# Down weights of the experts in rows of 16 KB over two ring slots, and inner features in neighbouring pairs

## What is computed

```python
def expert_block(args):
    xblk, e = args                       # tokens routed to expert e
    hid = jax.nn.silu(xblk @ w_gate[e]) * (xblk @ w_up[e])   # w_gate, w_up: 1024 x 512
    return hid @ w_down[e]                                   # w_down: 512 x 1024
...
y = jnp.zeros((t, d), xf.dtype).at[sorted_tok].add(contrib)  # weighted by the router, 2 experts a token
```

## Time and profile before

| | us |
|---|---|
| median of three runs (2711.89 to 2713.6) | 2712.69 |
| the profiled execution's own time | 2713.97 |
| its span, first to last instruction | 2712.2 |
| TensorE busy in the span | 2504.5 (92%) |
| VectorE busy | 1291.7 (48%) |
| ScalarE busy | 866.9 (32%) |
| mean traffic of the DMA engines | 263 GB/s |

### The profile page before, as it was taken

One profiled execution on the slowest core, in us unless ns is written; L12 is line 12 of the kernel. 1 busy time (PEld: TensorE's weight loads), 2 busy tenths in 40 slices (PEclk: granted clock), 3 DMA queues, 4 the chain that ended last, 5 costly groups with the idle time before them and its releaser, 6 DMA issues.

```text
span 2712.2 us, 39463 instructions
## 1 busy us (share of the span) xinstructions
PE 2504.5 (92%) x16084; PEld 1855.5 (68%) x16085; DVE 1291.7 (48%) x2254; ACT 866.9 (32%) x1474; POOL 294.3 (11%) x376
## 2 busy tenths in 40 slices
PE   7999899988898988998899999989999999989998
PEld 4664433443784433343699888879989988888997
DVE  6563323222664323221554675565455467555545
ACT  3241111110342111110344444444444444444443
POOL 0210100000000010000000212320010011233001
PEclk9989999999998999999899999999999999999999
DMA  9987999999774999999755444335646544334372
GB/s 390 343 323 320 420 419 418 412 420 418 242 280 198 420 420 419 414 420 420 278 200 185 143 125 136 124 124 198 197 155 202 187 137 156 119 116 154 132 240 79
DMA packets 253288, 712.09 MB, mean 263 GB/s; under 512 B 14514, under 2 KB 171954, under 8 KB 196786
## 3 DMA queue, kind: packets, MB, share of 16 engines
q1 hardware_dynamic: 249474, 704.94, 68.9%
q10 hardware_dynamic: 2208, 2.60, 0.3%
q0 software_dynamic: 1424, 1.98, 0.2%
HBM read 705.52 MB, written 1.05 MB: 261 GB/s over the span
## 4 chain that ended last, share of the span: by engine, by line
PE 62%; DMA 22%; issue 6%; DVE 5%; POOL 2%; ACT 2%; SPq 1%; ACTq 0%; DVEq 0%; POOLq 0%
DMA ring<-in_e_w_up_dram 19%; PE w L869 17%; PE w L1131 11%; PE y L909 9%; PE w L871 9%; DMA ring<-in_ada_w_dram 3%; PE w L1150 2%; PE w L1417 2%; PE y L776 1%; PE y L1183 1%; DVE wsp L1526 1%; POOL arena L2820 1%; PE w L1402 1%; PE w L971 1%; ACT wsp L1516 1%
## 5 line engine op out<-in xcount | busy, mean ns | idle before, releaser
L1526 DVE TENSOR_TENSOR wsp<-ring,wsp 128x1024 fp32r<-128x1024 f32 x470 | 578.8, 1237 | 400.8 <-ACT wsp L1516 400.3
L869 PE MATMUL w<-hh,wsp 128*128 128x256 f32 (+1 forms) x4800 | 634.0, 285 | 1.0 <-DVE wsp L1526 0.6
L869 PEld LDWEIGHTS w<-hh,wsp 128*128 128x128 f32 (+1 forms) x4800 | 602.8, 191 | 24.4 <-issue 11.9
L1516 ACT CAST wsp<-ring 128x1024 fp32r<-128x1024 f32 x470 | 487.9, 1045 | 389.1 <-PE w L871 208.5
L1131 PE MATMUL w<-ring,arena 128*64 128x512 f32 x2016 | 461.4, 600 | 85.1 <-DMA ring<-in_e_w_up_dram 80.1
L1131 PEld LDWEIGHTS w<-ring,arena 128*64 128x64 f32 x2016 | 154.9, 137 | 353.0 <-issue 351.2
L871 PE MATMUL w<-hl,wsp 128*128 128x256 f32 (+1 forms) x2400 | 336.6, 283 | 0.0
L871 PEld LDWEIGHTS w<-hl,wsp 128*128 128x128 f32 (+1 forms) x2400 | 309.5, 192 | 0.0
L909 PE MATMUL y<-wsp,zsp 128*128 128x512 f32 x1104 | 267.0, 391 | 4.1 <-DVE wsp L1526 3.8
L2012 DVE TENSOR_TENSOR ht<-w,ht 128x256 f32<-128x256 f32 x64 | 39.5, 617 | 450.9 <-ACT ht L2549 450.9
L2549 ACT ACTIVATE ht<-w 128x256 f32<-128x256 f32 x64 | 40.0, 625 | 635.7 <-PE w L1131 635.7
(11 more groups left out here) (345 smaller groups left out, 2522.6 us busy)
## 6 DMA issues: line engine op xcount, KB each, us to landing
ring<-in_e_w_gate_dram SPq DMA_DIRECT2D x126, 1024.0 KB, 8.6
ring<-in_e_w_up_dram SPq DMA_DIRECT2D x126, 1024.0 KB, 10.8
ring<-in_e_w_down_dram SPq DMA_DIRECT2D x124, 1024.0 KB, 12.0
ring<-in_ffn_in_dram SPq DMA_DIRECT2D x88, 1024.0 KB, 5.4
ring<-in_w_in_dram SPq DMA_DIRECT2D x50, 1024.0 KB, 5.2
ring<-in_ada_w_dram SPq DMA_DIRECT2D x48, 1024.0 KB, 12.2
ring<-in_ffn_out_dram SPq DMA_DIRECT2D x44, 1024.0 KB, 5.1
ring<-in_b_w_in_dram SPq DMA_DIRECT2D x12, 1024.0 KB, 10.1
```

Source lines behind the costliest of these rows:

```text
L869: pe.matmul(dst, a[:, kc * m:(kc + 1) * m], hh[:, kc, :], start=kc == 0 and j == 0, stop=False)
L1516: ac.copy(shaped(halves(i)[0], u.shape), u.cut(ring[:, u.piece % NSLOT, :])).then_inc(*mark("w_high", i))
L1526: ve.tensor_tensor(shaped(lo, u.shape), u.cut(ring[:, u.piece % NSLOT, :]), shaped(hi, u.shape).bitcast(F32), ALU.subtract).then_inc(*mark ...
```

## The change

The two down pieces of experts 1 to 30 become one DMA of 2 MiB over two neighbouring slots, an even slot and the next. Partition p now holds rows 4p to 4p + 3 of the matrix, one contiguous run of 16 KB. The DMA waits until both slots are free. TensorE's two halves of `down` both wait on this one DMA, and `ring_read` is raised once, after the second half. Expert 31's down matrix still comes in two pieces and expert 0's in the two early buffers; these are now two of the four rows of a partition each, 8 KB a run as before, at a pitch of 16 KB.

With rows 4p + k in partition p, `he` must hold features 4q + k. The gate and up pieces stay as they were in memory, but `up` now takes its columns in neighbouring pairs: half c takes features 4q + 2c and 4q + 2c + 1, so the moving operand is 256 runs of 2 floats, 16 bytes from one run to the next, where it was 2 runs of 256 floats. The output bank is written without gaps as before, and the patterns of L2549 and L2012 don't change.

```diff
-                    wanted.extend(("down", l, e_ - 1, h) for h in range(2))
+                    wanted.append(("down", l, e_ - 1))
...
+        def wide_piece(key, src):
+
+            n = len(pieces)
+            assert n % 2 == 0
+            piece_of[*key, 0] = piece_of[*key, 1] = n
+            pieces.append({"wide": src, "units": [], "read": n})
+            pieces.append({"units": [], "read": n})
...
-                _, l, e_, h = w
-                src = I["e_w_down"][l, e_, 256 * h:256 * h + 256, :]
+                _, l, e_ = w
+                src = I["e_w_down"][l, e_].rearrange("(p k) n -> p k n", p=P)
...
+                elif e_ < E - 1:
+                    wide_piece(w, src)
+                else:
+                    for h in range(2):
+                        piece_of[*w, h] = len(pieces)
+                        pieces.append({"parts": [(lambda r: r.rearrange("p (k n) -> p k n", k=2), src[:, 2 * h:2 * h + 2, :])], "units": []})
...
+        def half_pairs(two, k, c):
+
+
+            return two.rearrange("p u (k q c j) -> p k c u q j", k=4, c=2, j=2)[:, k, c]
+
+        def as_pairs(a):
+            return a.rearrange("p (u q j) -> p u q j", u=2, j=2)
...
+                if n >= NSLOT and ("wide" in piece or "parts" in piece):
+                    slot_free(n - NSLOT)
+                if "wide" in piece:
+                    slot_free(n + 1 - NSLOT)
+                    sp.dma_start(two_slots(n % NSLOT), piece["wide"]).then_inc(*mark(f"ring{n % NSLOT}", n, by=16))
...
-                                ins = pe.matmul(b[64 * c:64 * c + 64, :], xg[:, u, kc, x0:x0 + CAP], r4[:, k, :, 256 * c:256 * c + 256],
+                                ins = pe.matmul(as_pairs(b[64 * c:64 * c + 64, :]), xg[:, u, kc, x0:x0 + CAP], half_pairs(two, k, c),
                                                 start=kc == 0, stop=kc == KC - 1)
...
-                            w = ring[:, np_ % NSLOT, :].rearrange("p (k n) -> p k n", k=2)
+                            w = ring[:, (piece_of["down", l, e_, 0] + h) % NSLOT, :].rearrange("p (k n) -> p k n", k=2)
...
-                        if e_:
+                        if e_ and (h == 1 or np_ != piece_of["down", l, e_, 1]):
                             ins.then_inc(*mark("ring_read", np_))
```

More of the change, by code:

```diff
@@ L568, in program @@
             elif w[0] == "down":
-                _, l, e_, h = w
-                src = I["e_w_down"][l, e_, 256 * h:256 * h + 256, :]
+                _, l, e_ = w
+                src = I["e_w_down"][l, e_].rearrange("(p k) n -> p k n", p=P)
                 if e_ == 0:
[L572 to L575, removed]
+                    early[l].extend((early_down[h].rearrange("p (k n) -> p k n", k=2), src[:, 2 * h:2 * h + 2, :], "in_taps")
+                                    for h in range(2))
+                elif e_ < E - 1:
[4 more added lines that the diff above has]
+                        pieces.append({"parts": [(lambda r: r.rearrange("p (k n) -> p k n", k=2), src[:, 2 * h:2 * h + 2, :])], "units": []})
         assert len(units) == len(unit_list)
@@ L707, in late, with slot_free @@
                                     sp.sem_inc(s_, 1)
+            def slot_free(n):
+                if pieces[n]["units"]:
+                    for i in pieces[n]["units"]:
+                        sp.wait_ge(*low_done(i))
+                else:
+                    sp.wait_ge(*at("ring_read", pieces[n].get("read", n)))
             def early_loads(l):
@@ L741, in sync_engine @@
                     sp.dma_start(xa[:, :, :], I["x"][0].rearrange("(t p) d -> p t d", p=P)).then_inc(*mark("in_x", 0, by=16))
[L742 to L748, removed]
+                if n >= NSLOT and ("wide" in piece or "parts" in piece):
[3 more added lines that the diff above has]
+                    sp.dma_start(two_slots(n % NSLOT), piece["wide"]).then_inc(*mark(f"ring{n % NSLOT}", n, by=16))
+                for view, src in piece.get("parts", ()):
                     sp.dma_start(view(ring[:, n % NSLOT, :]), src).then_inc(*mark(f"ring{n % NSLOT}", n, by=16))
@@ L1126, in up @@
                             two = ring[:, np_ % NSLOT - 1:np_ % NSLOT + 1, :]
-                        r4 = two.rearrange("p u (k n) -> p k u n", k=4)
                         for k in range(4):
@@ L1146, in down @@
                             pe.wait_ge(*at(f"ring{np_ % NSLOT}", np_))
-                            w = ring[:, np_ % NSLOT, :].rearrange("p (k n) -> p k n", k=2)
-                        for c in range(2):
+                            w = ring[:, (piece_of["down", l, e_, 0] + h) % NSLOT, :].rearrange("p (k n) -> p k n", k=2)
+                        for j in range(2):
                             for dh in range(2):
-                                ins = pe.matmul(b[64 * dh:64 * dh + 64, :], he[:, i, c, h, :], w[:, c, 512 * dh:512 * dh + 512],
-                                                start=h == 0 and c == 0, stop=h == 1 and c == 1)
-                        if e_:
+                                ins = pe.matmul(b[64 * dh:64 * dh + 64, :], he[:, i, j, h, :], w[:, j, 512 * dh:512 * dh + 512],
+                                                start=h == 0 and j == 0, stop=h == 1 and j == 1)
+                        if e_ and (h == 1 or np_ != piece_of["down", l, e_, 1]):
                             ins.then_inc(*mark("ring_read", np_))
@@ L1276, in late @@
                                         for dh in range(2):
[L1277 to L1278 removed]
+                                            ins = pe.matmul(WB[3][64 * dh:64 * dh + 64, :], he[:, 0, c, h, :],
+                                                            two_slots(4)[:, 2 * h + c, 512 * dh:512 * dh + 512], start=(h == 0 and c == 0),
                                                             stop=(h == 1 and c == 1))
```

17 lines of the change are left out of this document (9 added, 8 removed).

## The result

| | before | after |
|---|---|---|
| median, us | 2712.23 (6 runs, 2710.04 to 2713.6) | 2727.22 (6 runs, 2721.39 to 2730.69) |
| ratio to before | | 1.0055 [1.0043, 1.0067] |
| span of the profiled execution | 2712.2 | 2725.6 |

A forecast was written before the change was run, and what follows sets the result against it. Transfers were taken to bound the expert layers, with TensorE 10% behind. Gains of 2.2 us a layer, cut to 0.9 by the wait at each layer's end, took the profiled 2713.97 to 2712.2, a median of 2711; range 2704 to 2724.

The forecast's parts named there:

- What bounds the kernel: Expert layers: transfers set the pace at 14.97 us an expert; TensorE is 10% behind, with 1.5 us to spare.
- One down DMA in place of two: DMA engines: 16 KB rows save 77 ns a matrix, 2.2 us a layer; bounds nothing and 4.4 us.
- SyncE and the slots: Down DMA issued later, at about 406.3, with 6.3 us of cover; the later issue costs nothing.
- TensorE's wait for 2 MiB: First half of `down` starts 1.45 us later; the wait replaces old waits of `up` and costs nothing inside a layer.
- the DMA cover above: Gate and up pieces queued ahead of the down DMA, 6.3 us, said to absorb a lateness of 1.3 us.
- experts with extra work: Experts where TensorE has almost no slack; the DMA cover was to take up their 1.3 us lateness.
- The end of a layer: At `down(30)` the wait isn't hidden: 0.87 us earlier instead of 2.2; without row saving, 1.35 us later.
- The sum: Whole kernel: 2713.97 less 0.9 a layer gives 2712.2 profiled, 2711 median; 2715.4 without saving, 2706.5 with double saving.
- The moving operand in pairs: `up` reading 8 bytes of every 16 was costed at nothing, provided an instruction reads a column once.
- Both forms of the rival: Pairs slow `up`: columns read twice, about 3060 us; or 2.4 ns per 16 bytes, about 2765; chance 0.17.
- The rivals: Pairs slow `up`, 0.17; longer rows save nothing or cost a little, 0.2; merged DMA saves more than rows show, 0.15.
- signs of being wrong: `up` over 4.4 us a half with DMA share under 1, or landings further apart than 14.97 us.

The follow-up runs named there:

- wide from expert 23 on: Changed kernel with the merged down DMA in 16 KB rows only at experts 23 to 29, two 1 MiB DMAs elsewhere, pairs kept; 2714.7 us, 1.0008.
- the light kernels: Kernel before and changed kernel, both with `combine` at 2 of 8 matmuls and gathers without the low-order half; 2709.64 and 2716.71 us.
- the light changed kernel: Changed kernel with `combine` cut to 2 of 8 matmuls for all but first and last pairs, gathers without low-order half; 2716.71 us, 1.0011.

## Why the prediction was wrong

**What bounds the kernel.** Right on average and misleading in single experts. The spare time of 1.5 us an expert is a mean over 26; the earlier trace rows can't show single steps. Before, TensorE is idle for 0.0 us in steps 1 and 17 of both layers and for less than 0.5 in steps 2, 3, 5, 21 and 23, and for 1.0 to 3.2 in nearly all others.

**One down DMA in place of two.** Right in mechanism and size. The rows aren't cut: the page counts 8639 packets fewer, and 60 matrices with 128 rows and 16 closing packets fewer are 8640. The page of the kernel before has

```profile
DMA packets 253288, 712.09 MB, mean 263 GB/s; under 512 B 14514, under 2 KB 171954, under 8 KB 196786
```

The step fell from 14.96 to 14.88, 0.08 us a matrix where I had 0.077. But a cheaper transfer shortens a body only if nothing else lengthens it: with the merged DMA in 8 KB rows and in 16 KB rows the time is the same (2721.66 and 2721.61), and in the changed kernel the gain shows clearly only in steps 26 to 29.

**SyncE and the slots.** The late release costs nothing, as forecast: 1.0000 with it alone. The sentence after it was wrong: "`up` moves by at most 1.3 us, so I cost the later issue at nothing". The gate and up pieces come up to 2 us closer to their turn, as the timeline after shows.

**TensorE's wait for 2 MiB.** This is the step that failed. "The new wait takes the place of old ones" holds in the sum of waits, and "the DMA cover above takes up a lateness of 1.3 us" doesn't hold. I had reckoned the cover from the median gate piece of the whole run (8.6 us from issue to landing, 2.5 its own), and applied it to experts in which TensorE is already behind. There TensorE's 1.3 us for the wait, and 0.3 us an expert for the pairs, push the reads of gate and up back until the queue behind the down matrix is short, and what the DMA engines don't move then is not made up, since they were the bound. That the wait costs 10 us where I had 2.7 is shown by the kernel with the wait alone. A long step by itself costs nothing: with the wait alone, steps 5, 7, 15, 21 and 23 take 16.1 to 16.2 us, and the steps after all but the first of them, 13.7 to 14.2, make it up to within 0.5 us. Clear losses stand where the DMA rate falls, in step 17 above all (382 GB/s before, 373 with the wait alone, 366 in the changed kernel) and in the first steps. So "experts with extra work" is too wide a name for the place: it is where the spare time is gone and the queue already short. The kernel that is wide from expert 23 on agrees with this; the light kernels, whose distance is half, agree in part. That it is the late gate and up issues which leave the queue short is read from the timelines and windows above; no kernel changed those issues by themselves.

**The end of a layer.** The mechanism was right. The wait costs 1.5 us an end where I had 1.35, and the changed kernel shows 1.2 and 1.1. The 2.2 us that were to be gained ahead of it never came, so there was nothing to pay from.

**The sum.** The 29 steps I had at 2.2 us less a layer; they are 2.9 and 4.1 more. Of the 13.4 us between the two spans, steps 1 to 4 hold 3.0, 5 to 16 1.0, 17 to 25 3.6, 26 to 29 0.7 less, the ends 2.3. The other 4.1 lie in stretches that the change doesn't touch. These take 1795.3 us in the profile before, and from 1790.7 to 1799.4 over the profiles of all kernels; so a single profile doesn't account for all of the 15 us, and the size rests on the medians.

**The moving operand in pairs.** Costed at nothing; it costs 0.15 us a half, and 2 us in the whole kernel by the medians, which is within the bound. Both forms of the rival, 3060 us with each column read twice and 2765 us at the price of 2.4 ns, are out. On top of the wait the pairs may cost more: 1.0055 with and 1.0040 without them, and the intervals overlap. They do take TensorE's time where it is short, and that is an argument, not a result.

**The rivals.** None of the three described what happened, and the slower side that I named, pairs that slow `up`, wasn't the cause. Of the signs of being wrong that I named, landings further apart than 14.97 us came (15.78), and a half of `up` over 4.4 us didn't (3.82). The wait that decided stands in my text as a step with a cost of nothing; it should have been the rival.

**Still open** is what the light changed kernel loses in its first four steps (1.5 us a layer), how the loss splits between the steps of a layer beyond step 17, and why the pairs seem to cost more on top of the wait. No kernel that ran was faster than the kernel before beyond the bound of measurement.

## What to carry to other kernels

Merging two transfers into one makes its first reader wait for the whole; before that is priced at nothing, read the spare time of the reader step by step and not over a stretch, and look for steps in which the queue is short already. A ring whose slots are freed by a busy engine can turn a small lateness of that engine into idle transfer engines. A longer step with a shorter one behind it costs nothing; the loss is where the transfer rate falls. The cheap test is to add the wait alone to the kernel before: three lines told 10 of the 15 us.

## What the runs showed of the hardware

A row of 16 KB goes as one packet and costs 0.08 us less a matrix of 2 MiB: 6.29 MB in 14.88 us is 423 GB/s, where 8 KB rows gave 420. Matmuls whose moving float32 operand has 8 bytes of every 16, in two column strips, take 3.82 us for 16, 4.1% more than the 3.67 without gaps. The Trainium skill ("SBUF — State Buffer", Door 1), by which two hits in a 16-byte line are enough for full bandwidth, is near to that, and the measured number decides.
